# Early rows for four experts instead of two, and a turned-chunk order by twos, in the mixture of experts of a two-layer decoder trunk

## Chip, cores and metric

One core of one Trainium2 chip. The time is device microseconds of one execution of the whole program; times of a kernel are medians of some executions. The engines are TensorE (PE; its weight loads are PEld), VectorE (DVE), ScalarE (ACT), GpSimd (POOL) and SyncE (SP). SP, ACT and POOL each issue transfers on a DMA queue of their own (q1, q10, q0), and all queues share 16 DMA engines.

## The reference

Input is x, 512 tokens of 1024 float32. Two layers follow: a mixer (compressed, selected and windowed attention in layer 0; latent attention in layer 1), then a mixture of 64 experts in 8 groups. Only the latter matters here:

```python
h = rmsnorm(x, norm_ffn[i]).reshape(B * S, D)
grp = argmax(softmax(h @ w_group + b_group))
top_p, top_i = top_k(softmax(logits of the 8 experts of grp), 2)
weights = g_w * top_p / sum(top_p)
# assignments are sorted by expert; each expert's rows:
ys = (silu(xb @ w_gate[e]) * (xb @ w_up[e])) @ w_down[e]     # 1024 -> 256 -> 1024
x = x + sum over a token's two experts of ys * weight
```

So 1024 assignments are spread over 64 experts, 16 each on average. An expert's three matrices are 3 MB, and all 64 are read from memory in each layer.

## The kernel before, in words

**Phases.** The program runs mixer 0, experts 0, mixer 1, experts 1 in one instruction stream per engine. The end of a mixer and the routing are interwoven: `project_out` (PE, from L1366) makes the output product of each of four tiles of 128 tokens, turns the sum, makes the router's logits (`logits`, L1212) and counts picks (`count_tile`, L1226). DVE's side of it is `add_output` (L2120), which runs `pick_tile` (L1795) for each tile: top group, top two experts, and `pick[:, 2, t, :]`, a row of 64 zeros and ones for each token.

**Counting.** `count_tile(t)` makes two products in bank 6: L1229 counts, within the tile, the tokens below each token that took the same expert (64 columns), and L1232 adds the tile's totals to all later tiles and to the grand total, with 256, 192, 128 and 64 columns for t = 0 to 3. Once the fourth is done, `route` (DVE, L1830) makes `pair_hot` (L1837, 512 elements per partition): for the experts 0 and 1, a one-hot of each token's rank. PE's eight small products (L1407) turn that into the token number of each place of the two experts, written as BASE minus the sum of `token_left`, so that an empty place names token 1000, which is out of bounds. DVE's L1845 makes `token_pair` from it.

**Early rows.** POOL's `moe_moves` (L758) issues an indirect load of 128 rows (64 places for each of experts 0 and 1, 4 KB a row) from `token_rows` into the space of the last chunk. Places out of bounds are skipped (L766). Meanwhile DVE goes on with the sort: every assignment's place among the 1024 sorted rows, its inverse by L1245, and `token_of` (L1874). POOL then issues eight indirect loads (L771), one for each chunk of 128 sorted rows; the last one waits until the early rows have been turned.

**PE's order in the experts (`moe_pe`, L1242).** Turn the early chunk (`turn_rows`, L1284: 16 transposes of 64x64 pieces into two banks), one filler product (`keep_busy`), up products of experts 0 and 1 (`up`: 32 matmuls at L1187), down of 0, turn all eight sorted chunks, down of 1, up of 2, and from there a loop of up(n+1), down(n). A down is a transpose of the hidden rows (L1262), ACT's copy of it (L918) and 8 matmuls (L1196). ACT and DVE copy a half of each turned chunk (`chunk_half`, L920 and L1999); a pair of banks is free for chunk c once the copies of chunk c-2 are made.

**DVE's order (`moe_dve`, L1972).** Blocks of experts 0 and 1 from the early chunk (L2013), then `block_tables` and `share_weights` (30 small operations), the joins of hidden rows 0 and 1 (L1976), `keep_rows` of expert 0 (L1983, L1984), eight chunk copies, blocks 2 and 3 (L1994), `keep_rows` of expert 1, then the loop. `keep_rows` hands an expert's result to POOL, which scatters it (L788).

**Weights.** The arena has 7 slots of 3 MB. The weights of experts 0 to 6 are loaded before the first product, the last 3 MB of them when the last normed rows are written (L579 to L582). Then the SP queue reloads slots as they come free (L584 to L598): for slots 0 to 3 in two parts, 2 MB after the up product and 1 MB after the down product, strictly in the order up 0, down 0, up 1, down 1 and so on; for slots 4 to 6 and in the loop, 3 MB after the down product:

```python
for u in range(PARTED):                       # 0 to 3
    sp.wait_ge(up_done, done + u + 1)
    part(SLOTS + u, u, 0, 2).then_inc(weights_loaded[u], 16)
    sp.wait_ge(down_done, done + u + 1)
    part(SLOTS + u, u, 2, 3).then_inc(down_part_loaded[u], 16)
for u in range(PARTED, SLOTS):                # 4 to 6
    sp.wait_ge(down_done, done + u + 1)
    expert_weights(sp, l, SLOTS + u, u)
```

## Time and profile before

| | |
|---|---|
| median of 3 runs | 1625.5 us (1623.71 to 1628.79) |
| the profiled execution's own time | 1631.93 us |
| its span, first to last instruction | 1630.2 us |
| mean granted TensorE clock | 0.990 of full |
| busy: PE, DVE, ACT, POOL | 1437.2, 607.3, 340.9, 248.9 us |
| q1 (weights and other SP transfers) | 450.17 MB, 66.0% of 16 engines' span |

The page cuts the span into 40 slices of 40.75 us; the experts of layer 0 fill slices 11 to 22, those of layer 1 slices 29 to 40. A window row gives the busy time of each engine in a stretch, the granted TensorE clock (1.00 is full speed, 0.50 half) and the share of the 16 DMA engines in use (it can read slightly over 1). The chain that ended last is followed back from the last instruction; each of its pieces is what the next one waited for.

### The profile page before, as it was taken

To read this page: it belongs to the slowest core of one execution; us is meant where nothing else is said; L and a number is where in the kernel's file an instruction comes from. 1 tells how busy PE (TensorE), PEld (TensorE's weight loads), DVE (VectorE), ACT (ScalarE), POOL (GpSimd) and SP (SyncE) were. 2 spreads that over 40 slices of the span, in tenths; PEclk is the share of its full clock that TensorE was granted. 3 is DMA by queue.
4 is the path that set the end of the run, shared out by engine and by line. 5 is a ranking of instruction groups with operands and counts; after the bars stand their busy time and mean duration, and the time that the engine had idled before them with its cause. 6 is when DMAs were issued, how large, how long until landed. Compare 5 with 4: busy or idle time off the path is not lost.

```text
span 1630.2 us, 24202 instructions
## 1 busy us (share of the span) xinstructions
PE 1437.2 (88%) x8999; PEld 900.5 (55%) x8999; DVE 607.3 (37%) x1523; ACT 340.9 (21%) x983; POOL 248.9 (15%) x293
## 2 busy tenths in 40 slices
PE   8999999999899988787778999999899977778785
PEld 3655466655566655555555555655566655555453
DVE  2145677742532222212123556423522222222225
ACT  2122377741110000000001345412100000000000
POOL 1122100000211111111112233000211111111112
PEclk9999999999999999999999999999999999999998
DMA  7115140026699999999999401473899999999997
GB/s 294 47 52 209 50 156 1 1 119 236 240 365 430 429 429 429 429 430 430 429 430 421 184 1 78 181 297 116 340 393 426 430 429 428 429 430 430 428 430 297
DMA packets 44661, 480.91 MB, mean 295 GB/s; under 512 B 11262, under 2 KB 11790, under 8 KB 24944
## 3 DMA queue, kind: packets, MB, share of 16 engines
q1 hardware_dynamic: 28144, 450.17, 66.0%
q0 software_dynamic: 15296, 25.61, 4.5%
q10 hardware_dynamic: 1152, 4.19, 0.6%
q8 instruction: 45, 0.74, 0.2%
q14 instruction: 24, 0.20, 0.0%
HBM read 462.37 MB, written 47.19 MB: 313 GB/s over the span
## 4 chain that ended last, share of the span: by engine, by line
PE 57%; DMA 33%; DVE 6%; issue 2%; ACT 1%; another core or an unknown queue 0%; POOL 0%; SPq 0%; DVEq 0%; ACTq 0%; POOLq 0%
DMA sb_arena<-moe_w 32%; PE ps L1187 12%; PE ps L1381 7%; PE ps L1602 7%; PE ps L1196 7%; PE ps L1708 2%; PE ps L1738 2%; PE ps L1723 2%; PE ps L1568 2%; PE ps L1428 2%; PE ps L1456 2%; PE ps L1452 1%; PE ps L1288 1%; PE ps L1509 1%; PE ps L1539 1%
## 5 line engine op out<-in xcount | busy, mean ns | idle before, releaser
L1187 PE MATMUL ps<-sb_arena,sb_x_block 128*64 128x256 f32 x4096 | 473.5, 384 | 89.2 <-DMA sb_arena<-moe_w 88.7
L1187 PEld LDWEIGHTS ps<-sb_arena,sb_x_block 128*64 128x64 f32 x4096 | 419.9, 197 | 196.4 <-issue 133.5
L1196 PE MATMUL ps<-sb_arena,sb_hidden_space 128*64 128x512 f32 x1024 | 247.9, 605 | 46.0 <-ACT sb_hidden_space L918 45.6
L788 POOL DMA_INDIRECT expert_rows<-sb_y_sb,sb_row_now x124 | 133.2, 1074 | 733.0 <-DVE sb_y_sb L1984 665.7
L1983 DVE COPY sb_row_now<-sb_row_of 128x1 uint32 (+1 forms) x124 | 19.1, 154 | 601.3 <-PE ps L1196 586.8
L918 ACT COPY sb_hidden_space<-ps 128x128 f32<-128x128 f32 x128 | 34.1, 267 | 762.6 <-PE ps L1262 757.0
L1196 PEld LDWEIGHTS ps<-sb_arena,sb_hidden_space 128*64 128x64 f32 x1024 | 62.1, 136 | 143.6 <-issue 73.7
L1381 PE MATMUL ps<-sb_sorted_rows,sb_arena 128*128 128x512 f32 x256 | 114.6, 594 | 2.1 <-DVE sb_arena L2226 1.3
L1994 DVE TENSOR_TENSOR sb_x_block<-sb_sorted_rows,sb_moe_gain 128x512 f32<-128x512 f32 x120 | 83.1, 693 | 23.2 <-issue 20.7
L1984 DVE COPY sb_y_sb<-ps 128x512 f32<-128x512 f32 x124 | 84.4, 681 | 0.0
L1381 PEld LDWEIGHTS ps<-sb_sorted_rows,sb_arena 128*128 128x128 f32 x256 | 46.9, 190 | 51.4 <-issue 48.8
L1137 ACT ACTIVATE sb_arena<-ps,sb_n_max_of 128x128 f32<-128x128 f32 (+3 forms) x128 | 66.5, 527 | 13.6 <-DVE sb_n_max_of L2402 13.5
L2402 DVE TENSOR_REDUCE sb_n_max_of<-ps 128x2 f32<-128x256 f32 (+1 forms) x64 | 52.6, 823 | 33.6 <-PE ps L1710 32.2
L1602 PE MATMUL ps<-sb_sorted_rows,sb_arena 128*128 128x512 f32 x128 | 57.1, 595 | 0.0
L1602 PE MATMUL ps<-sb_arena 128*128 128x512 f32 x128 | 57.0, 593 | 0.0
L1723 PE MATMUL ps<-sb_identity,sb_arena 128*128 128x128 f32 x320 | 46.2, 275 | 8.4 <-DVE sb_arena L2412 8.1
L1708 PE MATMUL ps<-sb_arena 64*128 64x128 f32 (+3 forms) x256 | 51.8, 482 | 1.2 <-ACT sb_arena L1085 0.7
L2412 DVE TENSOR_SCALAR sb_arena<-sb_arena,sb_n_weight 128x128 f32<-128x128 f32 (+3 forms) x128 | 51.4, 443 | 2.3
L822 POOL TENSOR_SCALAR sb_rstd<-sb_ssq 128x1 f32<-128x1 f32 x6 | 1.9, 310 | 321.1 <-ACT sb_hidden_space L866 321.1
L1149 ACT COPY sb_arena<-ps 128x256 f32<-128x256 f32 (+1 forms) x64 | 44.3, 693 | 30.6 <-PE ps L1723 29.4
L914 ACT ACTIVATE sb_hidden_space<-ps 128x128 f32<-128x128 f32 x128 | 35.9, 280 | 66.8 <-PE ps L1187 63.9
L1738 PE MATMUL ps<-sb_arena 128*64 128x128 f32 x640 | 49.1, 283 | 0.3 <-ACT sb_arena L1149 0.3
(316 smaller groups left out, 1496.7 us busy)
## 6 DMA issues: line engine op xcount, KB each, us to landing
sb_arena<-moe_w SPq DMA_DIRECT2D x116, 3072.0 KB, 38.0
sb_arena<-moe_w SPq DMA_DIRECT2D x10, 2048.0 KB, 7.7
sb_arena<-moe_w SPq DMA_DIRECT2D x16, 1024.0 KB, 6.2
sb_sorted_rows<-nsa_w_group SPq DMA_DIRECT2D x2, 2048.0 KB, 13.3
sb_arena<-nsa_w_group SPq DMA_DIRECT2D x2, 2048.0 KB, 7.8
sb_sorted_rows<-nsa_w_out SPq DMA_DIRECT2D x1, 4096.0 KB, 12.1
kept_rows<-sb_arena SPq DMA_DIRECT2D x8, 512.0 KB, 4.6
token_rows<-sb_arena ACTq DMA_DIRECT2D x8, 512.0 KB, 2.6
```

What stands on the lines that cost most here:

```text
L788: pool.indirect_dma_start(out=ys_dram.rearrange("r (j n) -> (r j) n", j=2), out_offset=bass.IndirectOffsetOnAxis(ap=row_now[:, u:u + 1], a ...
L1137: nc.scalar.activation(n_probs[:, s % 4, r, 0:n], ps[:, score_bank(s) + r, 0:n], ACT.Exp, bias=n_max_of[:, s % 4, r:r + 1], accum_out=n_su ...
L1187: last = nc.tensor.matmul(ps[j * BLOCK:(j + 1) * BLOCK, bank, 0:2 * P].rearrange("p (g n) -> p g n", g=2), x_rows[:, :, k], weights[:, 0:2 ...
L1196: last = nc.tensor.matmul(ps[j * BLOCK:(j + 1) * BLOCK, 2, :], hidT[:, c * BLOCK:(c + 1) * BLOCK], weights[:, 2, c * D + j * 512:c * D + ( ...
L1381: last = nc.tensor.matmul(ps[:, 4 + m % OUT_BANKS, :], hT_of[layer][:, k, t * P:(t + 1) * P], w[:, k, half * 512:(half + 1) * 512], start= ...
L1602: last = mm(ps[:, unit_bank(u), :], hT[:, k, t * P:(t + 1) * P], w[:, k, :], start=(k == 0), stop=(k == KD - 1))
L1708: mm(ps[:, bank + r, 0:n], qk_T[rows, g, c, t * P:n], qk_T[rows, g, 2 + kind, 0:n], start=True, stop=False)
L1723: last = nc.tensor.transpose(ps[:, 4 + r, j * P:(j + 1) * P], n_probs[:, s % 4, r, j * P:(j + 1) * P], ident[:, :])
L1738: last = mm(ps[r * DH:(r + 1) * DH, bank, t * P:(t + 1) * P], v_all[:, j, g, kind * DH:(kind + 1) * DH], n_probsT[:, s % 2, r, j * P:(j + ...
L1984: nc.vector.tensor_copy(y_sb[:, u, :], ps[:, 2, :]).then_inc(y_ready, 1)
L1994: return nc.vector.tensor_tensor(x_block[:, buffer].rearrange("p (a b) k -> p b a k", b=DEAL), rows.rearrange("p (b a) k -> p b a k", b=DEAL),
L2402: v.tensor_reduce(n_max_of[:, s % 4, :], ps[:, score_bank(s):score_bank(s) + 2, 0:n], AX, ALU.max, negate=True).then_inc(n_max, 1)
```

## The change

Experts 0 to 3 get early rows. Two indirect loads of 128 rows follow each other; both chunks are turned before the first product. An empty place now names token 511 and its row is loaded like any other (the bounds check is gone). The one-hots of ranks are made tile by tile (`mark_early`), those of the first three tiles during the mixer's end. `count_tile` no longer adds into later tiles: it multiplies the running sum of picks of the tiles before (`pick_sum`, made by DVE) and the tile's own picks, 64 columns each, and the grand total is made once, in bank 3. PE turns sorted chunks 0 and 1 after down 0, 2 and 3 after down 1, 4 to 7 after down 2. SP issues the 2 MB part after up u+1 before the 1 MB part after down u.

```diff
-        FIRST = 2
-        LAST_CHUNK = CHUNKS - 1
-        BASE = 1000.0
+        FIRST = 4
+        EARLY = 4
+        TURNS = CHUNKS + EARLY // 2
+        PAIRS_AT = CHUNKS - EARLY // 2
+        BASE = S - 1
...
-                for u in range(PARTED):
-                    sp.wait_ge(up_done, done + u + 1)
-                    part(SLOTS + u, u, 0, 2).then_inc(weights_loaded[u], 16)
-                    sp.wait_ge(down_done, done + u + 1)
-                    part(SLOTS + u, u, 2, 3).then_inc(down_part_loaded[u], 16)
+                for u in range(PARTED + 1):
+                    if u < PARTED:
+                        sp.wait_ge(up_done, done + u + 1)
+                        part(SLOTS + u, u, 0, 2).then_inc(weights_loaded[u], 16)
+                    if u >= 1:
+                        sp.wait_ge(down_done, done + u)
+                        part(SLOTS + u - 1, u - 1, 2, 3).then_inc(down_part_loaded[u - 1], 16)
...
-                pool.indirect_dma_start(
-                    out=xs_in(LAST_CHUNK), out_offset=None, in_=h_dram,
-                    in_offset=bass.IndirectOffsetOnAxis(ap=token_pair[:, :], axis=0),
-                    bounds_check=S - 1, oob_is_err=False).then_inc(rows_landed[LAST_CHUNK], 16)
+                for i in range(EARLY // 2):
+                    pool.indirect_dma_start(
+                        out=xs_in(PAIRS_AT + i), out_offset=None, in_=h_dram,
+                        in_offset=bass.IndirectOffsetOnAxis(ap=token_pair[:, i:i + 1], axis=0)).then_inc(rows_landed[PAIRS_AT + i], 16)
                 pool.wait_ge(token_ready, 2 * l + 2)
                 for c in range(CHUNKS):
-                    if c == LAST_CHUNK:
-                        pool.wait_ge(chunk_turned, l * (CHUNKS + 1) + 1)
+                    if c >= PAIRS_AT:
+                        pool.wait_ge(chunk_turned, l * TURNS + c - PAIRS_AT + 1)
...
-                pe.wait_ge(picks_ready, l * TILES + t + 1)
-                nc.tensor.matmul(ps[:, 6, t * EXPERTS:(t + 1) * EXPERTS], below[:, :], pick[:, 2, t, :],
-                                 start=(t == 0), stop=(t == 0))
-                later = TILES - t
-                last = nc.tensor.matmul(ps[:, 6, (t + 1) * EXPERTS:(TILES + 1) * EXPERTS].rearrange("p (t e) -> p t e", t=later),
-                                        ones[:, :], pick[:, 2, t:t + 1, :].to_broadcast([P, later, EXPERTS]),
-                                        start=(t == 0), stop=(t == TILES - 1))
-                last.then_inc(counted, 1)
+                if t >= 1:
+                    pe.wait_ge(hots_ready, l * (TILES + 1) + t)
+                if t >= 2:
+                    pe.wait_ge(picks_summed, l * 2 + t - 1)
+                if t >= 1:
+                    nc.tensor.matmul(ranks_at(t), ones[:, :], picks_until(t), start=True, stop=False)
+                pe.wait_ge(picks_ready, l * TILES + t + 1)
+                nc.tensor.matmul(ranks_at(t), below[:, :], pick[:, 2, t, :], start=(t == 0), stop=True).then_inc(counted, 1)
+                if t == TILES - 1:
+                    nc.tensor.matmul(totals, ones[:, :], picks_until(t), start=True, stop=False)
+                    nc.tensor.matmul(totals, ones[:, :], pick[:, 2, t, :], start=False, stop=True).then_inc(counted, 1)
...
                 def turn_chunk(c):
                     pe.wait_ge(rows_landed[c], landed(c, 2 * l + 1))
-                    if c == 0:
-                        pe.wait_ge(block_ready, base + 2)
+                    if c < 2:
+                        pe.wait_ge(block_ready, base + 2 * c + 2)
...
-                pe.wait_ge(rows_landed[LAST_CHUNK], 48 * l + 16)
-                turn_rows(LAST_CHUNK, 0)
+                for i in range(EARLY // 2):
+                    pe.wait_ge(rows_landed[PAIRS_AT + i], 48 * l + 16)
+                    turn_rows(PAIRS_AT + i, 2 * i)
                 keep_busy(1)
                 up(0, 0, 0)
                 up(1, 1, 0)
                 down(0, 0)
-                for c in range(CHUNKS):
+                turn_chunk(0)
+                turn_chunk(1)
+                up(2, 2, 0)
+                down(1, 1)
+                turn_chunk(2)
+                turn_chunk(3)
+                up(3, 3, 0)
+                down(2, 2)
+                for c in range(4, CHUNKS):
                     turn_chunk(c)
-                down(1, 1)
+                down(3, 3)
                 up(FIRST, FIRST, 0)
...
+            def mark_early(l, t):
+
+                dve.wait_ge(counted, l * (TILES + 1) + t + 1)
+                nc.vector.tensor_tensor(early_hot[:, t], col_no[:, 0:BLOCK].unsqueeze(1).to_broadcast([P, EARLY, BLOCK]),
+                                        ranks_at(t)[:, 0:EARLY].unsqueeze(2).to_broadcast([P, EARLY, BLOCK]), ALU.is_equal
+                                        ).then_inc(hots_ready, 1)
```

PE's eight small products become sixteen, by expert and then tile; only the fourth tile's wait for the last `mark_early`. DVE's order in the opening becomes: blocks 0 and 1, the tables, join 0, block 2, join 1, `keep_rows` 0, block 3, chunk copies 0 and 1, `keep_rows` 1, join 2, copies 2 and 3, `keep_rows` 2, join 3, copies 4 to 7, blocks 4 and 5, `keep_rows` 3, then the loop. ACT's copies of chunk halves are spread in the same way, each pair between an expert's gate and the copy of its turned hidden rows.

## Rows read from the trace of the kernel before

**Rows 1.** Windows, both layers: us, PE, PEld, DVE, ACT, POOL, clock, DMA share, GB/s.

```profile
462.00:468.00 6.00, 6.00 (x58) 5.67 (x58) 2.34 (x5) 0.28 (x1) 1.01 (x1) 1.00 0.80 251
468.00:483.00 15.00, 13.93 (x101) 9.11 (x99) 3.25 (x8) 1.44 (x6) 2.19 (x2) 1.00 0.97 391
483.00:486.00 3.00, 3.00 (x28) 2.47 (x26) 1.60 (x4) 0.00 (x0) 0.37 (x1) 1.00 0.79 217
...
500.00:880.00 380.00, 314.72 (x2196) 209.51 (x2196) 94.01 (x238) 26.66 (x108) 58.13 (x54) 1.00 1.01 429
1176.00:1180.00 4.00, 4.00 (x32) 2.85 (x30) 2.05 (x4) 0.00 (x0) 0.41 (x1) 1.00 0.40 100
...
1199.00:1202.00 3.00, 3.00 (x32) 2.81 (x30) 1.64 (x4) 0.00 (x0) 0.98 (x1) 1.00 0.82 240
1202.00:1590.00 388.00, 322.47 (x2256) 213.92 (x2254) 93.26 (x237) 27.55 (x111) 59.16 (x55) 1.00 1.01 429
```

**Rows 2.** The queue of SP around the release of slot 4.

```profile
483.80 0.33 SPq L538 DMA_DIRECT2D sb_arena<-moe_w  x1
```

**Rows 3.** Chain that ended last, layer 0: start, duration, what.

```profile
428.94 0.17 DVE sb_token_pair L1845
...
429.96 7.65 DMA sb_sorted_rows<-token_rows,sb_token_pair
437.66 2.10 PE ps L1288 x15
439.86 1.29 DVE sb_x_block L2013 x2
...
451.45 3.89 PE ps L1288 x64
...
462.18 7.01 PE ps L1187 x64
...
481.82 1.94 PE ps L1196 x8
```

**Rows 4.** The same chain, 1140 to 1206 us (layer 1).

```profile
1156.28 8.13 PE ps L1187 x64
```

**Rows 5.** Product engine in 355 to 427.5 us, by line and shape.

```profile
L1381 PE MATMUL ps<-sb_sorted_rows,sb_arena 128*128 128x512 f32 x128 | 57.3, 594 | 0.8 <-DVE sb_arena L2417 0.8
...
L1232 PE MATMUL ps<-sb_x_block,sb_sorted_rows 128*128 128x256 f32 x2 | 0.7, 407 | 0.0
```

**Rows 6.** DVE in order of time, routing and opening: start, duration, line.

```profile
427.76 0.69 DVE L1837 TENSOR_TENSOR sb_sorted_rows<-sb_sorted_rows,ps 128x512 f16<-128x512 f32 x1 [0.55 <-PE ps L1232]
...
429.01 0.41 DVE L1846 TENSOR_TENSOR sb_x_block<-ps,sb_count 128x256 f32<-128x256 f32 x1
...
451.57 0.68 DVE L1984 COPY sb_y_sb<-ps 128x512 f32<-128x512 f32 x1
```

**Rows 7.** POOL in order of time: the first indirect loads.

```profile
429.96 1.24 POOL L763 DMA_INDIRECT sb_sorted_rows<-token_rows,sb_token_pair  x1 [7.36 <-DVE sb_token_pair L1845]
...
435.54 0.94 POOL L771 DMA_INDIRECT sb_sorted_rows<-token_rows,sb_token_of  x1 [0.31 <-issue]
```

**Rows 8.** DMA queues in 434 to 437 us: packets, MB, share.

```profile
q1 hardware_dynamic: 123, 0.88, 69.8%
q0 software_dynamic: 169, 0.25, 28.0%
```

**Rows 9.** DMA queues in 437 to 450 us.

```profile
q0 software_dynamic: 1127, 4.08, 87.8%
```

**Rows 10.** Windows around the first products (columns as rows 1).

```profile
434.00:438.00 4.00, 0.95 (x8) 0.34 (x8) 0.00 (x0) 1.37 (x2) 2.88 (x3) 0.59 0.98 381
438.00:442.00 4.00, 4.00 (x26) 2.06 (x24) 2.08 (x6) 0.00 (x0) 3.05 (x4) 0.56 0.99 312
442.00:446.00 4.00, 4.00 (x39) 3.73 (x39) 3.48 (x18) 0.28 (x1) 1.65 (x2) 1.00 0.96 340
...
1154.00:1158.00 4.00, 3.53 (x10) 1.25 (x12) 2.33 (x8) 0.00 (x0) 3.08 (x4) 0.50 0.91 334
```

109 lines of the change are left out of this document (68 added, 41 removed).

## The prediction

> **What bounds the kernel now.** The forty slices come first: PE is busy throughout, but over most of both expert stages the DMA engines are at 0.9 or more. The windows then tell which of the two holds the time there. From 500 to 880 us and from 1202 to 1590 us the DMA share is 1.01 at 429 GB/s, while PE has idle time [rows 1]: the weight stream is the bound, and its end is where it last began to run without a gap, plus a fixed number of bytes. So the question is when that is. Before it the share falls below one: 0.80 in 462 to 468 us, 0.97 to 483, 0.79 in 483 to 486, and in layer 1 0.40 in 1176 to 1180 and 0.82 in 1199 to 1202 [rows 1]. The idle time is 1.2 + 0.45 + 0.6 = 2.3 us in layer 0 and 2.4 + 0.5 = 2.9 us in layer 1. The last gap of each ends with the reload of slot 4. SP issues it at 483.80 us [rows 2], right after PE's down product of expert 4, which runs 1.94 us from 481.82 us [rows 3]. From there a slot comes free about every 6 us and a load takes 3.1 MB / 429 GB/s = 7.3 us, so that the queue never runs dry again. The reader is to see in this that only one thing moves the end: **when PE finishes the down product of expert 4**. Everything up to there on PE's path counts one for one, in each layer, and the transfers in front of it do not, as long as they are done by then.
>
> PE's path to that point, by the chain of waits: the mixer's end and the routing up to DVE's token numbers at 428.94 us, the early rows' load (7.65 us from 429.96 us), the turn of the chunk at 437.66 us, the products, and eight turned chunks from 451.45 us [rows 3].
>
> **The change, step by step** (per layer; the positions are those of layer 0).
>
> *Counting.* The products that add a tile's totals have 256, 192 and 128 columns for tiles 0 to 2. Tile 0 loses its own, those of tiles 1 and 2 shrink to 64: 256 + 128 + 64 = 448 columns fewer. A 512-column pass costs 57.3 / 128 = 0.448 us [rows 5], so 448 columns in two passes are 0.78 us. In this stretch PE waits 0.8 us of 72 [rows 5], so it is PE's time: **-0.75**. The two new sums of picks and three early one-hots on DVE are some 0.3 to 0.4 us each and cost nothing: DVE waits for PE there (L1837's wait is itself on PE [rows 6]); without that cover they would cost 1.5.
>
> *Routing.* The one-hot after the last count has 256 elements in place of 512: a 256-element operation that reads PSUM takes 0.41 us, the old one 0.69 [rows 6]. It also waits for one product less. The sixteen small products in place of eight add a quarter of a microsecond beside DVE's scan. **-0.35** (0 to -0.5).
>
> *The early rows.* POOL issues a load every 1.25 us [rows 7], which is quicker than the DMA engines serve them, and the sorted chunks are issued later anyway. Two experts hold 32 rows on average, so 96 of the 128 places were skipped and are now loaded, and a second load of 128 follows. A packet of this queue takes 0.878 x 13 x 16 / 1127 = 0.162 us of one engine [rows 9], so the first load lands 96 x 0.162 / 16 = 1.0 us later (0.3 to 2: none of it shows in the trace of before), the second 128 x 0.162 / 16 = 1.3 us behind it. That 196 empty places read the same row is taken at the rate of other rows, with 2 as the upper bound on the first load and 2.6 on the second.
>
> While they load, the weight queue is served too: in 434 to 437 us it had 123 packets and the early queue 169 [rows 8], about one against one, and a skipped place took its turn like a filled one. The Trainium skill (DMA: Bandwidth & Descriptors, "Queues, rings and completion order") says that an engine drains a packet of some 9 to 17 descriptors from one queue before it switches. By that rule the early load would pass in one go, without the turns. What it would make of the time is the third rival.
>
> *The second turn.* The clock is low here: 0.59 and 0.56 of full in the two windows from 434 to 442 us, 1.00 after [rows 10]; in the second window that is 3.5 us at half speed, so it came back at 441.5 us. A turn from its first transpose to DVE's start on it took 2.1 us at half speed [rows 3]; eight take 8.0 us at full speed, 1.0 each. With the two gains above the first turn begins at 437.66 + 1.0 - 1.1 = 437.6 us, ends at 439.6, the second at 441.5, the filler at about 442.5 at full speed. Before, both products took 7.62 us from 440.74 us and two at full speed take 7.01 [rows 3], so at full speed they would have begun at 441.35. **+1.9 for these two steps, +1.15 with the gains taken off** in layer 0. In layer 1 the first two products took 8.13 us from 1156.28 us [rows 4], and the window before was at 0.50 to 1158 us [rows 10]; more of the added work is then beside a wait that was DVE's and not PE's: **+0.8 net**. If the clock is back where it was, more of the filler and first product runs at full speed, which is why 3.3 us of new work cost less.
>
> *Between the products.* The same six up products, five down products and eight turns lie before expert 4's down. Chunk 1's turn now waits for block 3, which DVE makes only after `keep_rows` of expert 0: 0.1 + 0.7 us [rows 6] and 0.65 for the block (half of 1.29 [rows 3]), 1.45 after the down, where the turn of chunk 0 takes 1.0: +0.45. In return, the pairs of chunks no longer wait for the copies of the pair before, three times of four: 0 to -0.4, taken at -0.25. **+0.2**. Queued behind DVE's waits for down 1 and down 2 are copies and joins that PE needs only an up product later, so they cost nothing; without that cover a copy of 0.7 would.
>
> *The weight queue.* The parts of slots 1 to 3 are issued several microseconds earlier. They fill gaps that lie before slot 4's release, and that is all. The early queue brings 224 more rows, 0.92 MB or 2.3 us of all engines, which those gaps and the later release take up (2.3 idle + 1.4 later in layer 0, 2.9 + 1.0 in layer 1). **0**; it would be 2.3 less the idle time if the gaps were gone.
>
> Sum: 1.15 + 0.2 + 0.8 + 0.2 = **+2.4 us**. The profiled execution took 1631.9 us, which would become 1634.3; it stands 6.4 above the median of the runs, 1625.5, to which the difference is carried: **1627.9 us**.
>
> **The rivals.**
>
> *1. The gaps were what cost time.* If an earlier release moved the end, all of 2.3 + 2.9 = 5.2 us would be won: 1620.3 us. For it: the share is under one for 20 us in each layer, and the reordered parts address just that. Against it: the last gap ends with slot 4 and not with a part [rows 2, 3]. Chance 0.09.
>
> *2. Slower: the clock stays low through the first product.* Place: the second turn and the first two products. PE's idle time ahead of the first turn is no shorter than before, and the work that follows is small transposes. If the clock is at 0.50 until the end of expert 0's up product, the product takes 7.0 in place of 3.5 us and filler and turn lose 1 to 2 more, of which 1 is in my sum: 3.5 a layer, 1627.9 + 7 = 1634.9 us; in one layer alone 1631.4. It decides as soon as the granted clock is below 0.75 in the two microseconds after the first product begins. Against it: the same stretch came back within 4 us in both layers before. Chance 0.20.
>
> *3. The loads are served in one go.* Each engine has nine packets of the early load, with a weight packet of 0.698 x 3 x 16 / 123 = 0.27 us before each [rows 8], 2.4 us in all, of which about half remains as the weights of that moment run out. Without it the turn begins 1.3 us earlier in each layer: 1627.9 - 2.6 = 1625.3 us. Against it are the nearly equal packet counts [rows 8]. Chance 0.08.
>
> *4. The step that was added hides itself.* If the second turn lies wholly beside DVE's dealing of the first blocks and the early rows land no later than before, only the gains of counting and routing stay, 2 x -1.1, with +0.2 each between the products: 1623.7 us. That the change does what it says is otherwise plain from its waits. Chance 0.10.
>
> **How the numbers follow.** My forecast has 0.53. A measurement of this kernel can tell about 0.3% (4.9 us) from no change, so faster is below 1620.6, slower above 1630.4. The forecast's own range, from the bounds of the landing (0.3 to 2), the turns and the copies, is 1624 to 1632; nine tenths of it count as same. Rival 1 gives faster, most of rival 2 slower, rivals 3 and 4 same. Faster 0.10, same 0.69, slower 0.21. The range reaches to rival 1 and nearly to the dearest form of rival 2: 1620 to 1634.
>
> **What would show it.** Right: the DMA share is 1.01 from the reload of slot 4 on, that reload is issued right behind expert 4's down product, 57 us after `token_pair` in place of 483.8 - 428.9 = 54.9, the early loads bring 256 rows, the count products take 0.8 us less by layer, and the gaps of 462 to 468 us are smaller while one of some 3 us stands before slot 4. Wrong: a DMA share near one from the first release, so that bytes bind; a first product that starts as long after `token_pair` as before; or a down product of expert 4 that comes earlier although the first product does not, which would mean that the turns between the products cost more than I have read.

## The result and the profile after

The changed kernel took 1635.55 us (median of 4 runs, 1633.61 to 1636.99) where the kernel before, timed beside it, took 1627.14: a ratio of 1.0049, interval 1.0031 to 1.0067. Timed once more in the study it took 1633.98 us against 1626.85, a ratio of 1.0052 (1.0035 to 1.0069). So it is slower by 0.5%, some 8 us, where 2.4 had been forecast and 1634.0 was the upper end of the range. Of the three answers, the forecast had given "slower by over 0.3%" 0.21. (Of a kernel further down, skip_once, two executions of 2114 and 2909 us fell in a slow state of the chip and are left out of its ratio.)

The windows of the changed kernel, columns as in [rows 1]; these answer to [rows 1] and [rows 10]:

```profile
434.00:438.00 4.00, 0.00 (x0) 0.00 (x0) 0.00 (x0) 0.35 (x1) 2.96 (x4) 0.55 0.93 352
438.00:442.00 4.00, 3.02 (x33) 2.42 (x34) 1.69 (x5) 0.00 (x0) 2.91 (x4) 0.50 1.01 385
442.00:446.00 4.00, 4.00 (x22) 2.18 (x22) 3.52 (x17) 0.00 (x0) 0.84 (x1) 0.67 1.02 418
...
462.00:468.00 6.00, 6.00 (x67) 5.11 (x65) 2.33 (x5) 1.17 (x2) 1.02 (x1) 1.00 1.03 437
468.00:480.00 12.00, 11.06 (x94) 6.56 (x96) 5.85 (x11) 2.96 (x7) 0.98 (x1) 0.86 0.96 394
480.00:486.00 6.00, 6.00 (x55) 5.23 (x52) 0.98 (x2) 0.28 (x1) 0.98 (x1) 1.00 0.50 184
486.00:490.00 4.00, 3.64 (x27) 2.40 (x28) 1.39 (x4) 0.45 (x2) 0.00 (x0) 1.00 0.39 92
...
500.00:880.00 380.00, 314.74 (x2204) 210.78 (x2202) 90.82 (x234) 26.54 (x107) 60.13 (x54) 1.00 1.01 429
...
1158.00:1162.00 4.00, 4.00 (x19) 2.14 (x20) 3.48 (x17) 0.00 (x0) 0.69 (x1) 0.57 1.04 420
1180.00:1199.00 19.00, 18.06 (x178) 14.11 (x176) 7.75 (x15) 4.03 (x10) 2.99 (x3) 1.00 0.94 371
1199.00:1206.00 7.00, 6.64 (x53) 4.67 (x50) 1.64 (x4) 0.45 (x2) 0.98 (x1) 1.00 0.37 115
1206.00:1590.00 384.00, 318.50 (x2228) 211.78 (x2224) 90.09 (x221) 27.52 (x111) 57.88 (x55) 1.00 1.01 429
```

Two things are to be seen. The gap that stood at 462 to 468 us (0.80 in [rows 1]) is gone: 1.03. In its place a wider one stands from 480 to 490 us (0.50 and 0.39: 3.0 + 2.4 = 5.4 us without transfers) and another from 1199 to 1206 us (0.37: 4.4 us). From there on the share is 1.01 at 429 GB/s as before. The parts were issued earlier, were done earlier, and the queues then stood still until slot 4 came free.

The queue of SP at that place, which answers to [rows 2]:

```profile
488.39 0.33 SPq L551 DMA_DIRECT2D sb_arena<-moe_w  x1
```

And the chain that ended last in layer 0, which answers to [rows 3] (start, duration, what; L1306 turns, L1257 is the filler, L1202 the up and L1211 the down product, L2049 the block of an early expert):

```profile
427.99 0.17 DVE sb_token_pair L1881
...
428.44 10.49 DMA sb_sorted_rows<-token_rows,sb_token_pair
...
438.98 2.21 PE ps L1306 x29
441.19 2.00 PE ps L1257 x2
443.19 7.78 PE ps L1202 x64
...
453.73 0.60 DVE sb_y_sb L2020
454.33 0.61 DVE sb_x_block L2049
...
455.07 1.10 PE ps L1306 x16
456.17 3.67 PE ps L1202 x32
...
475.25 3.63 PE ps L1211 x8
...
486.41 1.94 PE ps L1211 x8
```

In layer 1 (answers to [rows 4]) it is the second early load that the chain goes through:

```profile
1145.68 9.86 DMA sb_sorted_rows<-token_rows,sb_token_pair
...
1155.59 1.14 PE ps L1306 x15
...
1158.73 8.40 PE ps L1202 x64
```

Slot 4 is issued at 488.39 us, right behind expert 4's down product (486.41 + 1.94 = 488.35). Cut at the events on which the prediction rests, both traces read as below. The column "again" is the profile of the second timing of the same changed kernel, to show what differs from one execution to the next. All in us.

| | layer 0: before | after | again | layer 1: before | after | again |
|---|---|---|---|---|---|---|
| `token_pair` at | 428.94 | 427.99 | 427.39 | 1143.22 | 1143.85 | 1141.09 |
| to the first turn | 8.72 | 10.99 | 11.03 | 9.43 | 9.98 | 9.75 |
| to the first up product | 3.08 | 4.14 | 4.15 | 3.62 | 4.82 | 5.47 |
| to the end of expert 4's down | 43.02 | 45.22 | 43.15 | 42.85 | 44.16 | 42.87 |
| the three together | 54.82 | 60.35 | 58.34 | 55.91 | 58.96 | 58.09 |

What follows on the last event hardly moves. From the end of expert 4's down product in layer 1 to the end of the span it is 431.07 us before and 430.90 after, and 430.8 to 431.1 in all thirteen traces of this study in which slots 4 to 6 are reloaded in one piece. From the same event in layer 0 to layer 1's `token_pair` it is 1143.22 - 483.76 = 659.46 us before and 1143.85 - 488.34 = 655.51 after. Of the 4 us between them 0.6 are the counting of layer 1 (further down); the rest is the clock, which in the trace of before was short of full in the mixer of layer 1:

```profile
880.00:1140.00 260.00, 251.29 (x1150) 149.35 (x1147) 119.70 (x325) 94.27 (x269) 45.86 (x61) 0.99 0.40 159
```

The changed kernel has 1.00 in the same window. At a clock of 0.99 (0.987 by the two stretches in it, of 3.4 us at half speed each) 260 us lose 3.4. Without that accident the two spans, 1630.2 and 1633.7 us, would stand about 7 us apart, near what the medians say. The profile of before is untypical in a second place: count_two (below), which does the same from `token_pair` on, needs 54.39 and 54.90 us for the three rows together where before has 54.82 and 55.91.

### The profile page after: what moved, and what is told of

It is laid out like the page before. It is cut to its first block, busy times and chain, and to the rows that moved or that the text cites. A ratio compares the mean times of both kernels' runs of the same rounds, so it can differ in the third digit from the quotient of the medians.

```text
span 1633.7 us, 24293 instructions
## 1 busy us (share of the span) xinstructions
PE 1439.2 (88%) x9051; PEld 902.3 (55%) x9051; DVE 609.4 (37%) x1533; ACT 340.6 (21%) x983; POOL 251.9 (15%) x295
## 4 chain that ended last, share of the span: by engine, by line
PE 58%; DMA 34%; DVE 5%; ACT 1%; issue 1%; POOL 0%; SPq 0%; DVEq 0%; ACTq 0%
DMA sb_arena<-moe_w 32%; PE ps L1202 12%; PE ps L1408 7%; PE ps L1211 7%; PE ps L1632 7%; PE ps L1738 2%; PE ps L1768 2%; PE ps L1753 2%; PE ps L1598 2%; PE ps L1458 2%; PE ps L1486 2%; DMA sb_sorted_rows<-token_rows,sb_token_pair 1%; PE ps L1482 1%; PE ps L1569 1%; PE ps L1306 1%
## 5 line engine op out<-in xcount | busy, mean ns | idle before, releaser
L1202 PE MATMUL ps<-sb_arena,sb_x_block 128*64 128x256 f32 x4096 | 474.4, 384 | 89.4 <-DMA sb_arena<-moe_w 89.4
L1202 PEld LDWEIGHTS ps<-sb_arena,sb_x_block 128*64 128x64 f32 x4096 | 420.3, 197 | 195.1 <-issue 142.4
L1211 PE MATMUL ps<-sb_arena,sb_hidden_space 128*64 128x512 f32 x1024 | 249.6, 608 | 46.0 <-ACT sb_hidden_space L933 46.0
L1211 PEld LDWEIGHTS ps<-sb_arena,sb_hidden_space 128*64 128x64 f32 x1024 | 62.3, 136 | 144.2 <-issue 73.8
```

The costliest lines, as they stand in the source:

```text
L1202: last = nc.tensor.matmul(ps[j * BLOCK:(j + 1) * BLOCK, bank, 0:2 * P].rearrange("p (g n) -> p g n", g=2), x_rows[:, :, k], weights[:, 0:2 ...
L1211: last = nc.tensor.matmul(ps[j * BLOCK:(j + 1) * BLOCK, 2, :], hidT[:, c * BLOCK:(c + 1) * BLOCK], weights[:, 2, c * D + j * 512:c * D + ( ...
```

## The experiments

Sixteen runs follow, one of them the changed kernel again, with 6 to 12 executions each, beside 23 to 29 executions of the kernel before. The theory to be tested: the end is set by the end of expert 4's down product, which the change delays (a later landing, a second turn, longer low clock, the wait for block 3). The main rivals: bytes or PE set the end, the counting costs, the order of the reloads costs, or turning by twos costs.

### The four first: counting alone, filler, empty places

**count_two**: the kernel before with the change's counting by tile and routing alone, for two early experts.

```diff
 (kernel before)
-                later = TILES - t
-                last = nc.tensor.matmul(ps[:, 6, (t + 1) * EXPERTS:...], ones[:, :], pick[:, 2, t:t + 1, :]...)
+                    nc.tensor.matmul(ranks_at(t), ones[:, :], picks_until(t), start=True, stop=False)
...
+                mark_early(l, TILES - 1)
```

> The kernel before with the change's counting alone (narrow count products, running sum of picks, one-hots tile by tile), still early rows for experts 0 and 1 and everything after that as before. If PE's time at the mixer's end and the routing count one for one, 0.75 + 0.35 us a layer are won: about 2 us less than the kernel before (1 to 3), with the token numbers 1 us earlier in layer 0. Rival: the load of the early rows waits for the weights queued ahead of it, and nothing is won: 0 us.

Measured: 1626.64 us, ratio 0.9997 (0.9987 to 1.0006). `token_pair` came at 428.47 us, 0.5 earlier than in [rows 3], and expert 4's down product ended 54.39 and 54.90 us behind it. The 1 to 3 us that the theory expected didn't show: the interval allows a gain of 2.1 us at most. The counting does no harm. (Over all traces of the study `token_pair` of layer 0 lies at 428.8 to 429.5 us in the four with the old counting and at 427.4 to 429.1, mean 428.1, in thirteen with the new one for four experts: 1.0 us earlier. In layer 1 it comes 656.1 and 656.2 us behind expert 4's down product of layer 0 in the two traces with the old counting, one-piece reloads and an undisturbed mixer, and 655.3 to 655.7 in the eight with the new: 0.6 us earlier.)

**filler_before** and **filler_after**: more of PE's filler products while the early rows load, so that the clock stays up.

```diff
 (kernel before; in the changed kernel the second goes from 1 to 6)
-                keep_busy(3)
+                keep_busy(5)
...
-                keep_busy(1)
+                keep_busy(4)
```

> The kernel before with five filler products in place of three after the small products and four in place of one after the sort's, so that PE has work while the early rows load. Theory of the clock: the half-speed stretch of 6.8 us a layer goes, and with it half of the time from the first turn until the clock's return: 1.9 us in layer 0, about 2.8 in layer 1: 3.5 to 5 us less than before. Rival: the first product waits for DVE's blocks and the landing, not for PE's clock: within 1 us of before.

> The changed kernel with five filler products in place of three and six in place of one. Theory of the clock: the half-speed stretch of 10.2 us a layer goes; 5.7 us of turns, filler and product at half speed become 2.8 in layer 0, about as much or a little more in layer 1: 5 to 7 us less than the changed kernel, close to the kernel before. Rival: landing and DMA bytes bind, under 2 us less.

Measured: 1626.03 us, ratio 0.9992 (0.9983 to 1.0002), and 1635.0 us, ratio 1.0051 (1.0035 to 1.0068). Neither moved beyond its interval, where 3.5 to 7 us had been expected. The filler did hold the clock; the window of filler_before:

```profile
434.00:438.00 4.00, 3.57 (x12) 1.36 (x12) 0.14 (x2) 1.53 (x3) 2.87 (x3) 1.00 0.97 375
```

and yet the chain shows why little was won:

```profile
437.78 1.11 PE ps L1288 x16
438.99 1.29 DVE sb_x_block L2013 x2
...
447.77 0.30 DVE sb_hidden_space L1976
448.11 0.34 PE ps L1262
```

PE reached its first product a microsecond sooner (10.75 us after `token_pair` where it was 11.80) and then waited: DVE's chain from the first blocks through `block_tables` to the join of expert 0's hidden rows runs without a gap from 438.99 to 448.07 us and releases PE. In the kernel before, the same chain ended at 448.79 us, 0.4 behind the slow product; beside a fast one it is the path for longer. In both profiles with more filler, besides, a stretch of half clock came later (the clock of 1165 to 1200 us is 0.95 in both; it is so in 5 of the 16 others). The filler is therefore no test of what the low clock costs in the changed kernel.

**skip_after**: the changed kernel whose early loads skip empty places, as the kernel before did.

```diff
 (changed kernel)
-        BASE = S - 1
+        BASE = 1000
...
                         in_offset=bass.IndirectOffsetOnAxis(ap=token_pair[:, i:i + 1], axis=0),
+                        bounds_check=S - 1, oob_is_err=False).then_inc(...)
```

> The changed kernel with the bounds check and the token out of bounds for empty places again, so that only about 64 of the 256 early places are loaded. If the loads of empty places carry the loss, the first turn begins 1 to 2.5 us earlier and the second load lands with the first: 3 to 6 us less than the changed kernel in both layers together. Rival (second turn, clock and order carry it): under 1.5 us less than the changed kernel.

Measured: 1630.87 us, ratio 1.0020 (1.0009 to 1.0031): more than half of the loss is gone. Its chain:

```profile
429.38 7.85 DMA sb_sorted_rows<-token_rows,sb_token_pair
...
437.28 1.14 PE ps L1307 x14
...
438.43 1.14 PE ps L1307 x13
...
441.57 7.17 PE ps L1203 x64
```

The first turn comes 8.93 us after `token_pair` (9.54 in layer 1), where it was 10.99 (9.98): 2.1 and 0.4 us. As long as empty places are skipped, the second load costs the first almost nothing (8.93 us beside before's 8.72).

### Slot 4 and the order of the reloads

**parted_after**, **parted_before**, **parted_skip**: slots 4 to 6 are reloaded in two parts as slots 0 to 3 are, 2 MB when the up product has ended and 1 MB when the down product has. The first is the changed kernel, the second the kernel before, the third is skip_after. In the second the order on SP's queue is rewritten as well: the 2 MB of expert 1 go ahead of the 1 MB of expert 0, those of expert 3 ahead of expert 2's, and so on.

```diff
-PARTED = 4
+PARTED = 7
...
-        down_part_loaded = [sem(f"down_part_loaded{u}") for u in range(PARTED)]
+        down_part_loaded = [sem(f"down_part_loaded{u}") for u in range(4)] + kv_loaded[0:PARTED - 4]
...
 (parted_before alone)
-                for u in range(PARTED):
+                for kind, u in [('up', 0), ('up', 1), ('down', 0), ('down', 1), ('up', 2), ('up', 3), ('down', 2), ('up', 4), ('down', 3), ...]:
```

> The changed kernel with slots 4, 5 and 6 reloaded in two parts as slots 0 to 3 are: 2 MB when the expert's up product has ended, 1 MB when its down product has. Theory (the end is set by the release of slot 4, at the end of expert 4's down product, behind which the queues stood idle for 5.8 us in layer 0 and 4.4 us in layer 1): two thirds of slot 4's load start some 4 us earlier in each layer, the idle stretches fall to about 2 us, and the kernel takes 5 to 8 us less than the changed kernel, 1628 to 1631 us where the changed one takes 1635.5. Rival (TensorE's own row of products up to expert 6, or the bytes, sets the end, and the idle queues are only beside it): the gain is under 1 us, 1634.5 to 1636 us.

> The kernel before with the same two parts for slots 4, 5 and 6. Its queues stood idle for about 1 us ahead of slot 4's load in each layer and stood nearly still for longer while experts 0 to 3 were turned. Theory (release of slot 4): its up product ends some 2 to 4 us ahead of its down product, so up to 2 us a layer, 1623 to 1626 us against 1627. Rival (the load of slot 4 stands right behind those of slots 2 and 3, and the bytes bind): no gain, within 0.5 us of the kernel before.

> The changed kernel with both: empty places skipped in the early loads (1630.9 us by itself) and slots 4 to 6 in two parts. Theory: the two gains lie on one chain (the landing ahead of the first turn, and the end of expert 4), so they add up in part: 3 to 7 us below the kernel with empty places skipped, 1624 to 1628 us. If it stays above 1629.5 us, the end of expert 4's down product isn't what the parts relieve. Below 1625.5 us it beats the kernel before.

**sporder**: the changed kernel with the old order on SP's queue.

```diff
 (changed kernel)
-                for u in range(PARTED + 1):
+                for u in range(PARTED):
...
+                    sp.wait_ge(down_done, done + u + 1)
+                    part(SLOTS + u, u, 2, 3).then_inc(down_part_loaded[u], 16)
```

> The changed kernel with the old order of the reloads on SP's queue (up 0, down 0, up 1, down 1, ...), alone undone. In the change the second slot's first part goes ahead of the first slot's last. Theory (nothing waits for the moved parts; the queues have gaps anyway): within 0.7 us of the changed kernel, 1635 to 1636.3 us. Rival (the order of the reloads is a part of the loss): 1 to 3 us less than the changed kernel; or, if the new order helps, 1 to 3 us more.

Measured against the kernel before (1627.31 us beside them):

| | median | ratio |
|---|---|---|
| parted_after | 1627.86 | 0.9997 (0.9984 to 1.0010) |
| parted_before | 1624.21 | 0.9978 (0.9968 to 0.9987) |
| parted_skip | 1623.81 | 0.9974 (0.9962 to 0.9985) |
| sporder | 1637.39 | 1.0055 (1.0040 to 1.0069) |

Earlier reloading of slots 4 to 6 alone takes the changed kernel from 1.005 to 1.000: all of the loss, with PE's order of work left as it was. That bears out the theory's first half: not PE's path as such holds the time, but when it lets the weight queue go on. The windows of parted_after:

```profile
480.00:486.00 6.00, 5.64 (x45) 3.84 (x43) 0.98 (x2) 0.69 (x3) 0.00 (x0) 1.00 0.93 335
...
1192.00:1199.00 7.00, 6.64 (x55) 4.79 (x53) 1.25 (x4) 0.72 (x3) 0.00 (x0) 1.00 0.82 311
1199.00:1206.00 7.00, 6.64 (x53) 4.80 (x51) 2.40 (x7) 0.54 (x2) 0.98 (x1) 1.00 1.03 435
```

where the changed kernel had 0.50 and 0.37. With the earlier reload the span also ends sooner behind expert 4's down product: 427.6 us in parted_after and parted_skip, 428.3 in parted_before, where every kernel with one-piece reloads has 430.8 to 431.1. The kernel before gains 0.2% by the split and the new order on SP together: its smaller gaps ahead of slot 4 were on the path too, and what of it is the order alone wasn't run. In the changed kernel the old order is no better than the new (sporder, 1.0055 with an interval that covers the changed kernel's ratio; its median lies 1.1 us above what the theory allowed): the rival that the new order costs time is out.

### What of the delay is what

**loadempty**: the kernel before, its one early load filled with token 511 in empty places.

```diff
 (kernel before)
-        BASE = 1000.0
+        BASE = 511.0
...
-                    bounds_check=S - 1, oob_is_err=False).then_inc(...)
+                    ).then_inc(...)
```

> The kernel before, with the empty places of its one early load filled by token 511 in place of being skipped: the full 128 packets land, and nothing else changes. Theory (the packets of empty places delay the landing, about half of the change's later first turn): the first turn comes 0.5 to 1.5 us later in each layer than 8.7 and 9.4 us after its tokens are named, and the time rises by 1 to 3 us over the kernel before's 1627.1. Rival (the second load behind it is what delays the first, the empty places do nothing): the first turn comes within 0.2 us and the time stays within 0.7 us.

Measured: 1629.52 us, ratio 1.0011 (0.9999 to 1.0022), which is undecided by itself. The trace shows the place:

```profile
429.94 8.86 DMA sb_sorted_rows<-token_rows,sb_token_pair
...
438.85 1.14 PE ps L1287 x14
```

The first turn is 9.36 us after `token_pair` in place of 8.72, in layer 1 9.57 in place of 9.43: 0.6 and 0.1 us. Two things are in this. The load itself takes 8.86 us from its start, where it took 7.65: 1.2 us more (0.7 in layer 1, 9.09 in place of 8.43). And it starts 0.45 us after `token_pair` (429.49 to 429.94 us), where it started 1.02 us after [rows 3], since the indirect load is issued sooner without the bounds check: in layer 0 it is 0.44 or 0.45 us in all eight traces without the check and 1.02 or 1.03 in all ten with it.

A load counts as landed when sixteen marks have come, one for each of its parts; the kept traces have the time of each. In us from the start of the first early load:

| | layer 0: 15 parts landed | all 16 | layer 1: 15 parts landed | all 16 |
|---|---|---|---|---|
| skip_after | 7.55 | 7.85 | 7.98 | 8.54 |
| loadempty (one full load) | 8.85 | 8.86 | 8.89 | 9.09 |
| the changed kernel | 8.96 | 10.50 | 9.38 | 9.50 |
| the changed kernel again | 8.86 | 10.54 | 9.23 | 9.26 |
| filler_after | 8.84 | 9.43 | 9.67 | 10.12 |

So the second full load delays fifteen parts of the first hardly at all in layer 0 (0.0 to 0.1 us beyond loadempty). One part is late, and alone costs 1.5 to 1.7 us: in the six profiles with two full loads and the old filler the fifteenth part lands at 8.8 to 9.1 us and the last at 10.2 to 10.5. It is the same in the second load (439.31 us, then 440.00) and in a weight part that was under way (437.48, then 438.75). In layer 1 of the changed kernel no part stands out, and the landing is 0.2 to 0.4 us behind loadempty's. What holds the one part isn't shown. In these six profiles a packet of 16 KB of the instruction queue (q8) begins 8.0 to 8.3 us after the load's start and takes 0.92 us; in the changed kernel's queues of 434 to 437 us it is the last row:

```profile
q1 hardware_dynamic: 94, 0.66, 53.2%
q0 software_dynamic: 131, 0.48, 42.2%
q8 instruction: 1, 0.02, 1.9%
```

In filler_after, where that packet passes 2.9 us after the start, the last part is only 0.6 us behind. That fits such a packet in front of the one part, but no run moved it alone.

**block3**: the changed kernel, with block 3 made ahead of the copy of expert 0's rows on DVE (and PE's down product of expert 1 made to wait for the copy).

```diff
 (changed kernel)
                 up(2, 2, 0)
-                down(1, 1)
+                turn_hidden(1)
+                pe.wait_ge(y_ready, l * SENT + 1)
+                finish(1, 1)
...
                 join_hidden(1)
+                early_block(3)
                 keep_rows(0, 0)
-                early_block(3)
```

> The changed kernel with the block of expert 3 made ahead of the copy of expert 0's rows on VectorE, so that TensorE's second sorted turn doesn't wait for it (0.52 us in each layer in the changed kernel). Theory (the release of slot 4 sets the end, so each wait between the early products counts one for one): 0.7 to 1.2 us less than the changed kernel, 1634.3 to 1635 us. Rival (the wait is taken back before the eighth turn): nothing, 1635.2 to 1636 us.

**turns_once**: the changed kernel with all eight sorted chunks turned in one piece behind expert 2's down product. PE's down products of experts 1 and 2 are made to wait for the copy of the result before.

```diff
 (changed kernel)
-                turn_chunk(0)
-                turn_chunk(1)
                 up(2, 2, 0)
...
-                turn_chunk(2)
-                turn_chunk(3)
                 up(3, 3, 0)
...
-                for c in range(4, CHUNKS):
+                for c in range(CHUNKS):
```

> The changed kernel with its four early experts, but all eight sorted chunks turned in one piece after expert 2's down product, as the kernel before turns them after expert 0's. Theory (turning by twos gains nothing and costs the wait for block 3 and slower first products behind each turn, some 0.5 and 0.2 us each): expert 4's down product ends 0.5 to 1.5 us earlier after the tokens are named in each layer, 1632.5 to 1634.5 us. Rival (the turns by twos hide the copies of each other): the eight turns wait for copies as in the kernel before, and the time is 0 to 2 us above the changed kernel's 1635.5.

Measured: 1632.06 us, ratio 1.0030 (1.0021 to 1.0039), and 1632.44 us, ratio 1.0032 (1.0021 to 1.0043). block3 is better than the changed kernel by more than the theory's 0.7 to 1.2 us, turns_once lies at the lower end of its theory's range. The chain of block3 shows the wait gone, with both turns in one row right behind the down product:

```profile
451.28 1.94 PE ps L1211 x8
453.22 1.91 PE ps L1306 x32
455.13 3.67 PE ps L1202 x32
```

In the changed kernel PE's own row at this place was:

```profile
455.07 1.10 PE L1306 MATMUL ps<-sb_identity,sb_sorted_rows 64*128 64x64 f32 x16 [0.52 <-DVE sb_x_block L2049]
```

From the end of expert 0's down product to that of expert 1's it is 8.22 us where it was 8.86: 0.64 a layer, 1.3 in all. The rest of the 3 us goes with the clock. Each execution's mean granted clock is on record: it is 0.989 or less in 6 of 10 executions of the changed kernel and in 5 of 6 of sporder, but in 1 of 12 of block3 and in none of 10 of turns_once. Why the stretches at half speed come less often there isn't shown. And turning by twos has no use of its own: without it the kernel is as fast as with it and block 3 put right.

### Undone together

The changed kernel again, then two pairs undone together, then a combination of all.

> The changed kernel itself, timed again beside the others, since it had four runs so far and its parts are now judged against it by a few tenths of a per cent. Every theory expects 1634 to 1637 us, 1.004 to 1.0065 of the kernel before; below 1.004 the shares of the parts would be smaller than read so far.

**skip_b3**: skip_after and block3 in one. **skip_once**: skip_after and turns_once in one.

> The changed kernel with two things alone undone: empty places skipped in the early loads (1630.9 us by itself) and the block of expert 3 made ahead of the copy (1632.1 us by itself). Theory (each counts one for one on the way to expert 4's down product, so they add up: -4.7 and -1.3 to -3.1 us): 1627.8 to 1629.6 us, and what is left above the kernel before's 1627.1 is the second early turn and the slower first products behind turns, some 2 us a layer, less the gain of the quicker naming of tokens. Rival (they hide each other): 1630.3 us or more, as with skipped places alone.

> The changed kernel with empty places skipped and all eight sorted chunks turned in one piece after expert 2's down product. Theory (the turns by twos are worth nothing; the wait for block 3 is what they cost): the same as with places skipped and block 3 moved, within 0.8 us of it. Rival (turning by twos still saves copies' waits once block 3 is out of the way): 1 us or more above it.

Measured, beside 1626.85 us of the kernel before: after_again 1633.98 us, ratio 1.0052 (1.0035 to 1.0069); skip_b3 1629.36 us, 1.0016 (1.0006 to 1.0025); skip_once 1628.17 us, 1.0006 (0.9996 to 1.0017). With empty places skipped and the wait for block 3 avoided, some 5.5 us of the 8 are gone, and with the turns in one piece nothing that can be measured is left. What is undone adds up in part: -5 us for the places and -3 for the block singly, -6 together. The trace of skip_b3 has expert 4's down product end 55.17 and 55.82 us after `token_pair`, against 54.82 and 55.91 before; beside count_two's 54.39 and 54.90 it is 0.8 and 0.9 us later, which is most of the 2.5 us by which its median is still above.

**best** and **best_once**: skip_b3 and skip_once with slots 4 to 6 in two parts, and expert 3's last third issued ahead of expert 4's first part on SP.

```diff
 (SP's queue; the loop of the changed kernel, with PARTED = 7, has ('up', 4) ahead of ('down', 3))
-                for u in range(PARTED + 1):
+                for kind, u in [('up', 0), ('up', 1), ('down', 0), ('up', 2), ('down', 1), ('up', 3), ('down', 2), ('down', 3), ('up', 4), ('up', 5), ...]:
```

> All that relieved slot 4 together: the changed kernel with empty places skipped, slots 4 to 6 reloaded in two parts, the block of expert 3 ahead of the copy, and expert 3's last third issued ahead of expert 4's first part (in the kernel with both it stood on SP from 475.9 to 479.8 us behind a wait for the up product, with the queues at 0.86 to 0.89). Theory: the queues' idle stretches ahead of 486 us shrink by 2 us or more a layer, the time is 1620 to 1623 us, below the 1623.8 of the kernel with both and the 1627.1 of the kernel before. Rival (the up product of expert 4, which nothing here moves but by 0.5 us, now sets the end): 1622.7 to 1624.3 us.

> The best kernel so far (places skipped, slots 4 to 6 in two parts, expert 3's last third ahead of expert 4's first part; 1621.1 us, 0.996 of the kernel before) with the eight turns in one piece in place of by twos. Theory (what sets the end is how early the freed slots 0 to 6 are handed to the queues in sum, and the queues no longer stand still ahead of 500 us): within 1 us of 1621.1. Rival (release of expert 4's slot by its up product): the same time as well, but with an idle stretch ahead of that load. If the queues' idle time while the eight chunks are turned counts: 1 to 3 us above.

Measured: 1621.06 us, ratio 0.9960 (0.9946 to 0.9975), and 1620.93 us, ratio 0.9965 (0.9951 to 0.9979). Both beat both kernels. The windows of best, where the changed kernel had 0.50 and 0.37:

```profile
480.00:486.00 6.00, 5.64 (x43) 3.86 (x41) 1.55 (x4) 0.45 (x2) 0.00 (x0) 1.00 0.98 385
...
1192.00:1199.00 7.00, 6.29 (x48) 4.06 (x45) 1.64 (x4) 0.76 (x4) 0.98 (x1) 1.00 0.99 421
```

parted_before has half of this gain, 0.22%, with two early experts; the two intervals just touch (0.9946 to 0.9975 and 0.9968 to 0.9987). What the other half is isn't taken apart: best differs from parted_before in the four early experts and their reloads, in the counting (1.0 and 0.6 us earlier tokens) and in the place of expert 3's last third. parted_skip, in which that third still waits on SP behind expert 4's up product, is no better than parted_before (0.9974, within its interval), so that the four early experts by themselves aren't shown to gain anything.

## Why the prediction was wrong

The forecast had the right path and prices that were too low on it. Three of its steps failed: the return of the clock (taken at 441.5 us as before, measured at 444.6), the landing of the first load in layer 0 (1.0 us later, measured 2.3), and the balance of waits between the products (+0.2 us a layer, measured +0.4 and +1.0). A fourth error, in the price of a turn, went the other way.

**The frame was right.** "Only one thing moves the end: when PE finishes the down product of expert 4", and the change's earlier parts fill gaps that lie before and move nothing: the gap of 462 to 468 us closed and one of 5.4 us opened before slot 4, as the last part of the prediction had said with "some 3 us". The distance from that event to the end stayed at 430.8 to 431.1 us in thirteen traces. parted_after showed it by experiment. Rival 1 (the gaps were what cost time) falls with it, and rival 4 (the added step hides itself) too.

**Counting and routing**, forecast at -1.1 us a layer: measured -1.0 in layer 0 and -0.6 in layer 1. Near enough; single traces scatter by as much as 0.5.

**The clock is the step that cost most in the profiled execution.** The sum had "if the clock is back where it was, more of the filler and first product runs at full speed": back at 441.5 us, so that the filler takes 1.0 us and both products 7.01. In the changed kernel's profile the filler took 2.00 us and the stretch at half speed ended at 444.6 us, inside the first product. The mean granted clock of 430 to 450 us was, in the changed kernel, and then in skip_after:

```profile
430.00:450.00 20.00, 12.97 (x104) 8.80 (x104) 11.09 (x46) 1.88 (x4) 10.20 (x13) 0.74 1.00 391
```

```profile
430.00:450.00 20.00, 14.66 (x116) 9.89 (x116) 11.92 (x48) 2.33 (x6) 11.94 (x15) 0.83 1.00 394
```

It was 0.83 in the kernel before as well, and 0.74 in five of the six profiles of kernels that load two full batches with the old filler (the changed kernel, sporder, block3, turns_once, parted_after; 0.83 in after_again). A part of the low stretch falls on PE's wait and costs nothing. From the first turn on, 5.6 us of it lay on PE's work (438.98 to 444.6) where it had been 3.9 (437.66 to 441.5), in layer 1 7.6 in place of 5.7. Half of the difference is the price beside the kernel before: 0.9 and 1.0 us. Ahead of it PE had been idle for 5.41 us, where the kernel before had 3.05:

```profile
438.98 1.15 PE L1306 MATMUL ps<-sb_identity,sb_sorted_rows 64*128 64x64 f32 x16 [5.41 <-DMA sb_sorted_rows<-token_rows,sb_token_pair]
```

So the late landing is a likely cause of the late clock (skip_after, with the landing back, has 0.83 in layer 0), but after_again had the same idle time, 5.46 us, and 0.83: it isn't shown to be enough. Even there the low stretch ended at 443.1 us and the filler took 2.00 us.

Rival 2 had this mechanism at half of its price. Its condition was met in the changed kernel's profile: the low clock lasted into the first product, 0.67 in 442 to 446 us and 0.57 in 1158 to 1162 us. It wasn't met in after_again. The product took 7.78 and 8.40 us and not 7 + 3.5, so the price was about 0.9 us a layer and not 3.5. That the time it gave, 1634.9 us, is near the measured one is luck: the rest came from elsewhere.

A part of the rest is stretches at half speed that fall later. In the changed kernel's profile one fell on expert 3's down product, right behind the turned chunks: 3.63 us in place of 1.94. No term of the sum had that. How much this counts can be read from the executions, whose mean granted clocks are on record. Of the changed kernel three have 0.991 to 0.993 and took 1632.0 to 1632.3 us, seven have 0.988 to 0.990 and took 1633.6 to 1638.0. In parted_after it is the same: five at 0.992 or 0.993 took 1624.3 to 1626.3 us, six at 0.987 to 0.990 took 1627.9 to 1631.7. Of the kernel before, 10 of 105 executions beside the runs have 0.990 or less. So the changed kernel loses the clock more often; which of its steps brings that isn't isolated, but with block 3 alone moved only 1 of 12 executions is below 0.990, where 6 of 10 were.

**The landing is the second step that failed.** "The first load lands 96 x 0.162 / 16 = 1.0 us later, the second 1.3 us behind it": the first turn came 2.3 us later in layer 0 in both profiles, and 0.55 and 0.3 in layer 1. The price of the empty places was about right: 1.2 us in loadempty's load, 0.7 in layer 1. Two things were left out. The load starts 0.57 us sooner without its bounds check, a gain. And in layer 0 one of the sixteen parts of the load is 1.5 to 1.7 us behind the other fifteen, which had landed at about the time of one full load. The load itself became 10.49 - 7.65 = 2.84 us longer, beyond the upper bound of 2 us that the forecast had put on it.

**The second turn** was priced too high, which hid a part of this. The forecast read 2.1 us for a turn at half speed from the chain [rows 3], where the row runs on until DVE starts on the blocks. PE's own row of before has 1.15 us:

```profile
437.66 1.15 PE L1288 MATMUL ps<-sb_identity,sb_sorted_rows 64*128 64x64 f32 x16 [3.05 <-DMA sb_sorted_rows<-token_rows,sb_token_pair]
```

and both turns together took 2.2 us in the changed kernel (438.98 to 441.19). So the second turn added 1.1 us in layer 0. In layer 1 it had to wait for the second load (1155.59 us, the first had begun at 1153.84), and with the wait it added 1.2 and 1.9 us. (The recorded "+1.9 for these two steps, +1.15 with the gains taken off" doesn't agree with the gains of 1.1 us, with which it would be +2.25; the +1.15 follows from the positions, 442.5 - 441.35, and the sum uses that.)

**Between the products**, forecast at +0.2, is the third step that failed, though the row "to the end of expert 4's down" seems to bear it out: 43.02 and 42.85 us before, 43.15 and 42.87 in after_again. That row holds the first two products too, and these were quicker in after_again (7.4 and 7.2 us in place of 7.6 and 8.1). From their end to the end of expert 4's down product it was 35.4 and 34.7 us before and is 35.8 and 35.7 in after_again: +0.4 and +1.0. Of it 0.64 is the wait for block 3 with the copy ahead of it, which block3 takes back (35.2 and 35.1); that the pairs save 0.25 at copies has nothing to show for it, since turns_once without pairs has 34.9 and 34.8.

**The weight queue**, forecast at 0 for 0.92 MB more: the early queue brought more bytes in a span in which the queues stood still for 5.4 and 4.4 us anyway. That fits this kernel, and no run tests it for one without those gaps.

**The sum**, as differences from the profile of before. The naming is -1.0 and -0.6. After_again has in layer 0 +2.3 for the landing, +1.1 for the turn, -0.3 for the products and +0.4 between them, in layer 1 +0.3, +1.9, -0.9 and +1.0: +4.1 us in all. The profile of after has +2.3, +1.1, +0.2 and +2.0, then +0.55, +1.2, +0.3 and +1.0: +7.0 us. Both are too small by what before's profile has over count_two's (0.4 and 1.0 us), so that they stand for some 5.5 and 8.4 us. The medians and executions say the same: 1632.0 to 1632.3 us, the lowest three of after_again, are 5 above 1627, and the median of 1635.55 is 8.4 above. The forecast had 2.4. Of the 6 us that were missed some 1.4 are the reading of before's profile as a typical one, about 1 the waits between the products, and the larger part of the rest the clock; the landing's 1.3 us in layer 0 was partly made good by layer 1 (0.3 and 0.55 for 1.0) and by the overpriced turns.

**Rival 3** (loads served in one go) fell: the first turn came later, not earlier. Its rule in the Trainium skill (DMA: Bandwidth & Descriptors, "Queues, rings and completion order"), that an engine drains a packet of some 9 to 17 descriptors before it switches, isn't decided by the counts of queues here, 94 to 131 in 3 us; no run here shows it.

## What to carry to other kernels

When the bound is a stream that waits for freed buffers, find the last buffer at whose release the stream was dry, and ask of a change only what it does to that release; to free the earlier ones sooner only moves the gap. Here splitting the reload of slots 4 to 6 (0.2% on the kernel before, with a new order on SP; 0.5% on the changed one) was worth more than all reordering of the work in front. An added load that goes out right behind the one on the path may delay it little on most of its parts and still move its landing, since the last of sixteen parts decides: look at the marks of all parts before putting the delay down to bytes. And before taking differences from one profile, see from the times and clocks of the other executions how typical it is.

## What the runs showed that had not been expected

- Two full indirect loads issued 1.43 us apart: fifteen of sixteen parts of the first landed 8.96 us after its start, as with one full load (8.85), and the last at 10.50.
- The indirect load starts 0.45 us after its token numbers without the bounds check and 1.02 us after them with it.
- A skipped place isn't free of packets. With empty places skipped, the early queue of skip_after had more packets than the changed kernel in the same 3 us, and no more bytes (434 to 437 us):

```profile
q0 software_dynamic: 314, 0.45, 46.7%
```

  against 131 packets of 0.48 MB. In that view of skip_after 221 packets are under 512 bytes. With the places skipped the load takes 1.2 us less in layer 0 and 0.7 in layer 1 (before against loadempty).
- Filler work held the clock at 1.00 while the rows loaded, and the kernel wasn't measurably faster for it: 0.9992 (0.9983 to 1.0002). The product that ran at full speed ended before DVE's tables.
- Executions of one kernel lie in clusters that go with their granted clock (after_again: 1632.0 to 1632.3 us at 0.991 to 0.993, then 1635.7 to 1638.0 us at 0.988 and 0.989). One stretch of 3.4 us at half speed costs about 1.7 us where PE is on the path (3.63 - 1.94 in expert 3's down product).
